# Layers without a loop, earlier first roundings, and background products behind the transposes in a float32 two-block model

## The reference

```
for l in range(DEPTH):                       # 2 layers
    h = rmsnorm(h_res, norm_gain[l])
    u_pool, z_pool, c_q, c_kv, k_rope, z_mla, g_pool, g_mla = split(h @ w_in[l])
    y_pool = (pool_mix(u_pool, ...) * silu(z_pool)) @ pool_w_up[l]
    o_mla = mla(c_q, c_kv, k_rope, ...)      # 8 heads, causal, q and k normed per head
    y_mla = (o_mla * silu(z_mla)) @ mla_w_up[l]
    h_res = h_res + (sigmoid(g_pool) * y_pool + sigmoid(g_mla) * y_mla) @ w_out[l]
```

## Time and profile before

| | |
|---|---|
| median of 3 runs | 2193.45 us (2189.38 to 2195.34) |
| the profiled execution | 2198.28 us, its span 2196.4 us |
| mean granted clock of TensorE | 0.949 of full |
| busy: PE, PEld, DVE, ACT, POOL | 1983.7, 1595.0, 1292.2, 900.1, 283.8 us |
| attention of layer 0 | about 215 to 423 us |
| layer 0 ends, layer 1 begins | 571 to 578 us |
| second block begins | about 1126 us |
| its attention | about 1317 to 1474 us |

### The profile page before, as it was taken

How to read it: one execution, slowest core, us unless ns; L and a number is a source line. 1 busy time by engine, 2 the same in 40 slices (tenths; PEclk the granted TensorE clock), 3 DMA queues, 4 the chain that set the end, 5 groups by cost and what they waited for, 6 DMA issues and landing times. The chain is left out here.

```text
span 2196.4 us, 30295 instructions
## 1 busy us (share of the span) xinstructions
PE 1983.7 (90%) x11088; PEld 1595.0 (73%) x11088; DVE 1292.2 (59%) x1619; ACT 900.1 (41%) x1476; POOL 283.8 (13%) x211
## 2 busy tenths in 40 slices
PE   5998899999699979999989997879999997999994
PEld 4965678899696567879967684656556876777773
DVE  5449734344334974434448927765775335788886
ACT  3323333333232333333333325543665323777772
POOL 4120211100412022110041100100000000000001
PEclk9999889999799988999989999999999996999997
DMA  4201111132221111112312211012124243999995
GB/s 141 80 22 44 58 39 45 53 95 82 64 73 29 44 58 39 39 59 68 116 58 77 77 62 35 20 39 77 40 95 163 79 144 113 366 389 381 381 369 190
DMA packets 159892, 241.79 MB, mean 110 GB/s; under 512 B 8753, under 2 KB 106194, under 8 KB 159746
## 3 DMA queue, kind: packets, MB, share of 16 engines
q1 hardware_dynamic: 152370, 213.01, 28.7%
q0 software_dynamic: 4464, 16.25, 2.0%
q10 hardware_dynamic: 2912, 10.55, 1.2%
HBM read 223.55 MB, written 16.25 MB: 109 GB/s over the span
## 5 line engine op out<-in xcount | busy, mean ns | idle before, releaser
L759 PE MATMUL acc<-h_split,ring_split 128*128 128x264 f32 x1088 | 313.0, 288 | 0.0
L759 PE MATMUL acc<-h_split,v_split 128*128 128x264 f32 (+1 forms) x736 | 212.3, 288 | 10.0 <-DVE ring_split L1954 8.7
L759 PE MATMUL acc<-ring_split,v_split 128*128 128x264 f32 (+1 forms) x736 | 209.7, 285 | 0.0
L759 PEld LDWEIGHTS acc<-h_split,ring_split 128*128 128x128 f32 x1088 | 209.5, 193 | 0.0
L1954 DVE TENSOR_TENSOR ring_split<-ring,v_split 128x1024 fp32r<-128x1024 f32 (+1 forms) x78 | 92.5, 1187 | 173.2 <-ACT v_split L1360 173.2
L759 PEld LDWEIGHTS acc<-h_split,v_split 128*128 128x128 f32 (+1 forms) x736 | 138.8, 189 | 13.4 <-issue 13.4
L988 PE MATMUL acc<-h_split,ring_split 128*128 128x512 f32 x368 | 146.3, 398 | 0.0
L1949 DVE RECIPROCAL work<-work 96x528 f32<-96x528 f32 (+1 forms) x38 | 130.9, 3445 | 21.2 <-ACT work L1392 20.8
L759 PEld LDWEIGHTS acc<-ring_split,v_split 128*128 128x128 f32 (+1 forms) x736 | 138.9, 189 | 0.1
L759 PE MATMUL acc<-h_split,krope_split 128*128 128x264 f32 x320 | 97.2, 304 | 25.4 <-POOL ring_split L2583 20.3
L737 PE MATMUL acc<-latent,ring 128*96 128x264 f32 (+1 forms) x512 | 119.9, 390 | 0.0
(11 more groups left out here) (484 smaller groups left out, 5296.2 us busy)
## 6 DMA issues: line engine op xcount, KB each, us to landing
ring<-in_w_in SPq DMA_DIRECT2D x64, 1024.0 KB, 5.2
ring<-in_w_expert_gate SPq DMA_DIRECT2D x13, 2048.0 KB, 9.7
ring<-in_w_expert_up SPq DMA_DIRECT2D x12, 2048.0 KB, 11.0
ring<-in_w_expert_down SPq DMA_DIRECT2D x11, 2048.0 KB, 12.0
ring<-in_w_out SPq DMA_DIRECT2D x12, 1024.0 KB, 5.6
hres<-in_w_expert_down SPq DMA_DIRECT2D x5, 2048.0 KB, 10.0
hres<-in_w_expert_up SPq DMA_DIRECT2D x4, 2048.0 KB, 10.9
y_rows<-gate ACTq DMA_DIRECT2D x16, 512.0 KB, 7.1
```

Of the source, the lines that this page charges most:

```text
L759: ins = nc.tensor.matmul(dst[0:rows_, half, 0:HALF], w[:, k, :], x[:, c], start=(k == 0 and i == 0), stop=(k == last and i == 2), skip_gro ...
```

## The change

There are six parts.

1. The two layers are written out on each engine; waits are for constants, and the small increments of `held` behind a wait are gone.
2. `PLACE1` gives the pieces of weights other places in the ring.
3. `weights_upper(JOBS_B, 0)` and `(JOBS_B, 1)`, the roundings for ("z", 0) and its follower, stand ahead of heads 6 and 8 of the loop over heads, where they stood behind it.
4. In each step of both attentions, PE has the background product last. On ACT and DVE the order in a step stays.
5. ACT loads the table of the square root ahead of the output products.
6. The convolution goes from DVE to POOL, where a block takes four TENSOR_SCALAR and three TENSOR_TENSOR; POOL's copy of the block is gone.

```diff
-        PLACE1 = [0, 1, 2, 3] * 8
-        PLACE1[10], PLACE1[11] = 3, 2
+        PLACE1 = [0, 1, 2, 3, 0, 1, 2, 3, 0, 1, 3, 0, 2, 1, 3, 0, 2, 1, 3, 2, 1, 0, 2, 3, 0, 1, 2, 3, 0, 1, 2, 3]
...
-            with pe.Fori(0, LAYERS) as layer:
-                n.enter("layer", layer, LAYERS)
+            for n.layer in range(LAYERS):
...
                     if s < len(items):
                         scores(s)
-                    for x in background_at(s):
-                        back(x)
                     if s < 2:
                         rotq(HEADS - 2 + s)
                     if 2 <= s < len(items) + 2:
                         turn(s - 2)
                     if s >= 3:
                         values(s - 3)
+                    for x in background_at(s):
+                        back(x)
...
                 if s < len(items2):
                     scores2(s)
-                for c in background2_at(s):
-                    product3(("lx", c), act_evacuated, h2_up, h2_low)
                 if 2 <= s < len(items2) + 2:
                     turn2(s - 2)
                 if s >= 3:
                     values2(s - 3)
+                for c in background2_at(s):
+                    product3(("lx", c), act_evacuated, h2_up, h2_low)
...
                 for hd in range(HEADS + 1):
+                    if hd == HEADS - 2:
+                        weights_upper(JOBS_B, 0)
+                    if hd == HEADS:
+                        weights_upper(JOBS_B, 1)
...
-                for i in range(2):
-                    weights_upper(JOBS_B, i)
...
                 merged_upper(DC - 1)
+                nc.scalar.activation(small[:, 14:15], small[:, 1:2], ACT.Sqrt)
...
-            for s in range(STEPS2):
-                for c in background2_at(s):
-                    for j in range(TAPS):
-                        taps_at.setdefault(min(s + 1 + j, STEPS2), []).append((c, j))
...
-                for c, j in taps_at.get(s, ()):
-                    conv_tap(c, j)
...
-                pool.wait_ge(dve_made, at(dve_made, ("conv", c)))
-                nc.gpsimd.tensor_copy(lru_x[:, c, 0:S], tmp[2 + c % 2]).then_inc(pool_made, 1)
...
+                pool.wait_ge(act_evacuated, at(act_evacuated, ("lx", c)))
+                y, z = tmp[2], tmp[3]
+                for j in range(TAPS):
+                    x, w = lru_x[:, c, j:j + S], vec2[:, V_CW + 8 * j + c:V_CW + 8 * j + c + 1]
+                    if j == 0:
+                        chain(nc.gpsimd.tensor_scalar(y, x, w, vec2[:, V_CB + c:V_CB + c + 1], ALU.mult, ALU.add))
+                    else:
+                        chain(nc.gpsimd.tensor_scalar(z, x, w, None, ALU.mult))
+                        if j < TAPS - 1:
+                            chain(nc.gpsimd.tensor_tensor(y, y, z, ALU.add))
+                nc.gpsimd.tensor_tensor(lru_x[:, c, 0:S], y, z, ALU.add).then_inc(pool_made, 1)
```

More of the change, by code:

```diff
@@ L141, in __init__ @@
         self.inside = None
+        self.layer, self.before = None, {}
     def mark(self, sem, label=None, by=1):
+        if self.layer == 0:
+            self.before.setdefault(sem.name, self.value.get(sem.name, 0))
         self.value[sem.name] = self.value.get(sem.name, 0) + by
         if label is not None:
[L146 to L147 removed]
+            assert (sem.name, label, self.layer) not in self.marks, label
+            self.marks[sem.name, label, self.layer] = (self.inside and self.inside[0], self.value[sem.name])
     def enter(self, loop, index, trips):
@@ L174, in at @@
             return 1
-        loop, v = self.known.marks[sem.name, label]
-        return self._value(sem.name, loop, v, back)
-    def in_pass(self, sem, label, index):
-        if self.known is None:
-            return 1
-        loop, v = self.known.marks[sem.name, label]
-        return index * self.known.per[loop, sem.name] + v
+        marks = self.known.marks
+        if self.layer is not None and back and self.layer == 0:
+            return self.known.before[sem.name]
+        if self.layer is not None and (sem.name, label, self.layer) in marks:
+            return marks[sem.name, label, self.layer - back][1]
+        key = (sem.name, label, None)
+        loop, v = marks[key if key in marks else (sem.name, label, LAYERS - 1)]
+        return self._value(sem.name, loop, v, back)
     def now(self, sem):
@@ L605, in _ @@
             mark(vec_loaded, "vectors", 64)
-            with sp.Fori(0, LAYERS) as layer:
-                n.enter("layer", layer, LAYERS)
-                for i, (name, src) in enumerate(layer_granules(layer)):
+            for n.layer in range(LAYERS):
+                for i, (name, src) in enumerate(layer_granules(n.layer)):
                     slot = PLACE1[i]
@@ L1386, in _ @@
                 squares(c, ("x", c), ("sq0", c))
-            with act.Fori(0, LAYERS) as layer:
-                n.enter("layer", layer, LAYERS)
+            for n.layer in range(LAYERS):
                 def root(label, dst, width, rows_=P):
@@ L1939, in _ @@
             dve.wait_ge(dve_evacuated, at(dve_evacuated, ("x", DC - 1)))
-            with dve.Fori(0, LAYERS) as layer:
-                n.enter("layer", layer, LAYERS)
-                chain(nc.vector.tensor_copy(lv[:, :], vecs[:, bass.ds(layer * LV, LV)]))
+            for n.layer in range(LAYERS):
+                chain(nc.vector.tensor_copy(lv[:, :], vecs[:, n.layer * LV:(n.layer + 1) * LV]))
                 chain(nc.vector.tensor_copy(small[:, 8:9], lv[:, 21:22]))
@@ L2590, in weights_low_part @@
                          ("wlow",) + label)
-            with pool.Fori(0, LAYERS) as layer:
-                n.enter("layer", layer, LAYERS)
+            for n.layer in range(LAYERS):
                 weights_low_part(JOBS_A, 1)
```

43 lines of the change are left out of this document (11 added, 32 removed).

## The result

The changed kernel takes 2245.64 us (median of 4, 2241.51 to 2247.67) against 2193.47 us: a ratio of 1.0238, 95% interval 1.0218 to 1.0259. It is 52 us slower, on the side that was forecast and outside the range of 2172 to 2238.

What follows compares the result with a forecast made beforehand. PE was taken as the bound nearly everywhere (busy 1983.7 of 2196.4 us). Terms of -5 + 0 + 12 + 13 - 6 + 14 - 6 = +22 us on 2193.45 gave 2215 us, range 2172 to 2238.

Steps and rivals of the forecast that it cites:

- Copies late behind the tanh: First attention: ACT's copy of T stands behind the background product's tanh, so PE waits; +12 us (0 to 24).
- The normalisation held by POOL: First attention: T waits for DVE's normalisation, slowed beside POOL's rounding; +13 us (0 to 25).
- a term of 25: First attention, PE's new order: late copies at +12 us and late normalisation at +13 us.
- The clock: Rival: in the attentions the granted clock falls by another 0.03, some 17 us more, 2232 us; chance 0.15.
- the argument against the clock: Attentions: waits of 1 to 2 us stand in the kernel before without a fall of the clock.
- The loop boundary: Between layers 0 and 1: written out, the engines' slow start of the second turn goes; -5 us (-5.2 to 0).
- Early roundings: Before z0: PE's 10.15 us wait for POOL goes, but DVE paces what follows; 0 us (-3.4 to +4).
- Second attention: Second block's attention: -6 us for order without DVE taps, +14 for POOL beside DVE, -6 at its end.
- The intervals: Second attention, between background products: 18.3 us for four steps, plus about 2 us for POOL slowing DVE.
- The end: End of second attention: PE's 3.95 us wait for DVE's last taps and some slow clock go; -6 us (-7 to -4).
- POOL beside DVE: Second attention: POOL's convolution partly slows DVE's instructions, without a full lock; 2.0 us an interval, +14 us (0 to 28).
- The split into -6 and +14: Second attention: new order with DVE freed of taps gives -6 us, POOL's convolution slowing DVE costs +14 us.

Runs made afterwards that it cites:

- e2: Changed kernel with ScalarE's copies of T and V ahead of the background product's tanh in the first attention: 2230.23 us (1.0154).
- e9: Changed kernel with POOL's part of each weight in the first attention also waiting for the normalisation of the step behind the product: 2218.82 us (1.0102).
- e1: Changed kernel with PE's old order in the first attention, all else changed: 2182.78 us (0.9943).
- e10: Changed kernel with 41 additional, overwritten matmuls a layer ahead of T's wait for the normalisation in steps 3, 5, 19 and 30: 2221.13 us (1.0109).
- e12: Kernel before with its layers written out and nothing else: 2176.75 us (0.9905).
- e6: Kernel before with layers written out, new places in the ring and early square root table, nothing else: 2177.45 us (0.9933).
- e7: Changed kernel with PE's old order in both attentions and the convolution on DVE: 2179.29 us (0.9938).
- e5: Changed kernel with PE's old order in both attentions: 2174.82 us (0.9911).
- e11: Changed kernel with PE's old order in both attentions and the first roundings where they were before: 2168.61 us (0.9869).
- e16: Kernel with both old orders, late roundings and convolution on POOL, plus 24 additional matmuls ahead of z0 in each layer: 2169.41 us (0.9888).
- e8: Changed kernel with the background products z0 and z1 ahead of the rotation of q in steps 0 and 1: 2230.14 us (1.0169).
- e4: Changed kernel with the convolution back on DVE as taps and POOL's copy: 2245.83 us (1.0233).
- e3: Changed kernel with PE's old order in the second attention: 2232.83 us (1.0169).
- e15: Kernel before, loops and all, with only PE's new order in the first attention: 2231.1 us (1.0166).
- e13: Changed kernel with ScalarE's copies ahead of the tanh and POOL's part of a weight behind the normalisation: 2220.03 us (1.0118).

## Why the prediction failed

**The step that failed** is the pricing of waits in the first attention at their bare length, with the clock left out of the sum. The places were right. Copies late behind the tanh: 12 us forecast in the two layers, 12.6 us of waits found, 15 in time by e2. The normalisation held by POOL: waits of 1.8 and 2.5 us at steps 19 and 30, as replayed for 2.0, and e9 takes the first away. Even the idle time came near: 12.5 us a layer forecast, 14.5 and 13.3 more than before found. A part of that is luck. The 12.5 is net of 4 us for waits that go; gross it is 16.4, and T has 19.7 and 19.2. Missing were T(1), 3.6 us at step 3, which I had set against the early roundings at nothing, and waits of 1.1 us at steps 10 and 25; on the other side more of the old waits went than I took off. But I put no clock to the waits: e1 shows 17 and 16 us of idle time and 10 and 15 us of slower matmuls in the two layers, 63 us in all for a term of 25. The clock stood in the text as a rival at 17 us and 0.15; it belonged in the sum. e10 shows that the clock rises when waits are filled.

Two readings hid it. The earlier trace rows begin at 280 us and leave out the first 65 us of the attention, where PE is idle for 13.0 us and the clock is 0.83 in the kernel before:

```profile
214.90:280.00 65.10, 52.08 (x316) 41.94 (x315) 46.94 (x82) 24.14 (x66) 17.05 (x9) 0.83 0.16 49
280.00:422.80 142.80, 137.84 (x935) 115.16 (x934) 57.08 (x152) 52.67 (x165) 27.13 (x16) 0.94 0.13 40
```

And the argument against the clock, that waits of 1 to 2 us stand there without a fall, is not what that trace shows: the half clock from 272.0 us on (e12) sets in during a wait of 1.04 us, behind one of 0.67.

**The loop boundary** was forecast as -5 and is 5 us where I looked (0.15 us behind POOL's sum, e6 163.4 to 158.5). Writing out gives 17 us in all (e12), so that the term was 12 us short; the other 12 lie in the attentions. In the profiled executions the largest part of that is the stretch at half clock of 17.1 us in each layer (some 8.5 us a layer, an estimate from its length and its clock of 0.50, of the 9 to 12 that e6 gains). Why it comes is open: e6 has waits of 0.63 and 1.08 us at that place too, and no fall, and of the two layers of e12, equal in code, one has it.

**Early roundings**, forecast 0 (-3.4 to +4): 2 us (e7 against e6) to 6 us (e5 against e11) slower, the first within the noise. That z0 gains nothing, since DVE paces z1, was right, and e16 shows it from another side. Not foreseen was that in the new order z0 stands behind the rotation's wait, so that z1 comes 0.7 us later instead of 1.7 earlier. Putting z0 ahead of the rotation gives 15 us (e8), though PE waits as long.

**Second attention.** Forecast -6 + 14 - 6 = +2, measured +3.0 for the stage, and the intervals and the end hold too. The intervals: forecast +8 in all, measured 141.5 us from the first product to the last for 135.0 before. One of four steps: 18.3 + 2.0 = 20.3 forecast, 19.87 measured; of five, 23.3 and 22.86; e4's within 0.3 us of their replay. The end: forecast -6, measured 5.7 us from the last product to the next stage's for 10.7, -5. What I left out is that the first product comes 1.6 us later. The split into -6 and +14 is not tested: no run takes the taps off DVE without giving POOL the work. The order by itself costs 8 us (e1 against e5, and 8.0 in the stage in e3): four steps take 18.4 us with the old one, a loss of 1.4 us a time, and as much with the taps on DVE (20.2 in e4, 18.8 in e6). That the copy behind the product is this loss fits the replay but is not tested by itself.

**POOL beside DVE.** I kept to a partial slowing, 1.31 us for 0.75, from the earlier trace rows, and set the rule of an exclusive lock aside. That was a misreading of a mean. Of the eight DVE instructions three started before POOL's first and took 0.75 us each; the five others took 1.75 (shortest, median and longest: 747, 1752 and 1772 ns):

```profile
L2146 DVE SCALAR_TENSOR_TENSOR ring<-hres,vec,v x8: 747/1752/1772, 1132.5 to 1141.2; 128x512 f32<-128x512 f32 x8
```

In both traces, all 39 SCALAR_TENSOR_TENSOR on DVE with inputs in SBUF that started beside a TENSOR_TENSOR of POOL ended 0.55 to 0.57 us behind it, as in the place at 1461 us above. DVE's TENSOR_SCALAR does the same: 2.47 us beside POOL's 2.34, ending 0.16 us behind it, and 0.36 once POOL comes later (e9). Beside POOL's TENSOR_SCALAR of one operation (L2643), L2190, L2191 and L2199 lost 0.3 us or less, and they ended first unless POOL's had under 0.6 us to go. So it is POOL's instruction that decides here. The +14 rests on a wrong price: what the earlier trace rows show for a full overlap is a loss of 1.0 us, not 0.57, but over half of POOL's time in the convolution is in TENSOR_SCALAR (5.5 of 9.3 us a block), which takes less from DVE. The Trainium skill ("SBUF — State Buffer", "Who interferes with whom") states that when DVE is in a two-port mode, which tensor_scalar can be, the engine that issues first holds the shared ports for its whole instruction and the other one is blocked. It says there too that a DVE instruction with two inputs in SBUF contends with a GpSimd instruction that reads SBUF. This trace agrees with both beside POOL's TENSOR_TENSOR (2.47 for 0.36, 1.63 for 0.75), and not with a lock for the whole length beside L2643 (1.05 for 0.75, ended 0.34 us before POOL's).

**In sum**, from run to run: writing out -17 (e12), places and table +1 (e6), early roundings +2 (e7), convolution to POOL -5 (e5), second order +8 (e1), first order +63 (the changed kernel), together 52. The steps lead from the one kernel to the other, so that they must add up; another sequence gives other shares (37 for the first order in e15, 6 for the roundings in e11). Of the 30 us by which the forecast fell short, the first order's term is 38 too low and the loop's 12 too high, and the rest is small. The prediction would have been further off without the second error.

Open is what exactly makes the clock fall. Less idle time in e13 than in e9 went with a lower clock, e8 has a higher one than the changed kernel with as much idle time, and of the two equal layers of e12 one has 17 us at half clock that the other has not. So total idle time alone does not set it, and no run here separates what else does. For the same reason the gains of e2, e8, e9 and e10 can't be added.

## What to carry to other kernels

In a kernel that TensorE bounds, a new wait on it can cost nearly twice its length (59 us for 34 of idle time here, by e1), so look at the granted clock, stretch by stretch and from the stage's start, before adding up microseconds. A mean over instructions that overlap another engine's and ones that don't is the price of neither; look at the shortest and the longest. Here a long product was best placed between a short job and the one that waits for its result (e1), and each engine that evacuates should have its reads in the order in which the product engine makes them (e2). A hardware loop can cost more than its boundary: writing two turns out gave 0.7% to 1% (e6, e12), of which 0.2% lay at the boundary.

## What was not expected of the hardware

POOL's TENSOR_SCALAR on 128x512 took 1663 ns on average with one operation (1562 at the shortest) and 763 ns with two (multiply and add, L2641); its TENSOR_TENSOR took 1277. The one with two operations reads from column 0 and the others from columns 1 to 3, and no run tells whether the operations or the columns make the difference. DVE's TENSOR_SCALAR on two columns took up to 1.66 us beside POOL's TENSOR_TENSOR, for 0.17 alone. And 41 superfluous matmuls a layer made a kernel 24 us faster.
